# One stage in place of two at the head of a two-block transformer kernel: modulation product and first norm

## The reference, cut to what matters

```python
cond = jax.nn.silu(c)                      # c: 1 x 1024
mod = cond @ w_mod[l] + b_mod[l]           # w_mod: 1024 x 6144
shift_m, scale_m, gate_m, shift_f, scale_f, gate_f = [m[:, None, :] for m in jnp.split(mod, N_MOD, axis=-1)]
h = rms_norm(x, g_mix_norm[l]) * (1.0 + scale_m) + shift_m
x = x + gate_m * hybrid_mixer(h, positions, w_in[l], ...)
```

## Time and profile before

| | |
|---|---|
| median of 3 runs | 2143.41 us (2143.37 to 2143.73) |
| profiled execution | 2143.22 us, of which its span is 2141.5 us |
| `setup_stage`, from the span's start to the next stage's first instruction | 0 to 49.99 us |
| `norm_stage` mix1, in the same way | 49.99 to 72.01 us |
| `front1_stage`, in the same way | 72.01 to 213.06 us |

### The profile page before, as it was taken

The page is one execution under the profiler, slowest core; times in us unless marked ns, Lnnn a source line. Parts: engine busy times, 40 slices in busy tenths (PEclk is TensorE's granted clock), DMA queues, the critical chain, the costliest instruction groups (busy, mean ns, idle before and its releaser), DMA issues. The chain is left out here.

```text
span 2141.5 us, 28179 instructions
## 1 busy us (share of the span) xinstructions
PE 1873.8 (87%) x8588; PEld 1457.6 (68%) x8590; DVE 1321.0 (62%) x1543; ACT 1029.7 (48%) x1347; POOL 663.9 (31%) x510
## 2 busy tenths in 40 slices
PE   5778899997879999999999940789989878998999
PEld 2665676776758888888888830556666557887887
DVE  1692565454769999999999948364556654333332
ACT  0321344432248888888888831254555522222221
POOL 0498892000014666666666620011101100000000
PEclk9789899999689999999999975799999989999999
DMA  7644552211259999999999935432210003231222
GB/s 255 178 146 135 158 148 78 63 60 62 101 194 340 364 377 359 368 376 372 372 357 348 367 106 225 96 83 60 55 50 20 20 32 105 96 131 43 96 97 79
DMA packets 167507, 373.39 MB, mean 174 GB/s; under 512 B 39798, under 2 KB 77110, under 8 KB 158982
## 3 DMA queue, kind: packets, MB, share of 16 engines
q1 hardware_dynamic: 148614, 325.34, 44.2%
q0 software_dynamic: 18816, 47.04, 6.6%
HBM read 356.19 MB, written 29.23 MB: 180 GB/s over the span
## 5 line engine op out<-in xcount | busy, mean ns | idle before, releaser
L108 DVE TENSOR_TENSOR exp_parts<-exp_raw,exp_parts 128x2048 fp32r<-128x2048 f32 x194 | 439.3, 2291 | 57.6 <-ACT exp_parts L1872 57.2
L102 PE MATMUL ps<-exp_parts,xgT 128*128 128x512 f32 x1536 | 377.0, 401 | 7.6 <-DVE xgT L108 4.1
L1872 ACT CAST exp_parts<-exp_raw 128x2048 fp32r<-128x2048 f32 x194 | 369.0, 1918 | 14.9 <-PE ps L102 13.2
L102 PEld LDWEIGHTS ps<-exp_parts,xgT 128*128 128x128 f32 x1536 | 286.3, 190 | 77.3 <-issue 12.6
L102 PE MATMUL ps<-exp_parts,exp_hT 128*128 128x512 f32 x768 | 196.3, 405 | 2.7 <-DVE exp_hT L108 2.7
L102 PE MATMUL ps<-w_down_parts,hidden_parts 128*128 128x512 f32 x768 | 176.5, 392 | 7.1 <-DVE w_down_parts L108 7.1
L1767 POOL DMA_INDIRECT xg<-h_rows,row_index x63 | 147.4, 2340 | 108.9 <-issue 99.6
L102 PE MATMUL ps<-h4T,w_up_parts 128*128 128x512 f32 x768 | 175.8, 391 | 5.2 <-DVE w_up_parts L108 5.2
L102 PEld LDWEIGHTS ps<-w_down_parts,hidden_parts 128*128 128x128 f32 x768 | 145.7, 190 | 37.9 <-issue 7.5
L102 PEld LDWEIGHTS ps<-h4T,w_up_parts 128*128 128x128 f32 x768 | 145.2, 189 | 35.6 <-ACT w_up_parts L156 5.4
L102 PE MATMUL ps<-h3T,w_parts 128*128 128x512 f32 (+1 forms) x576 | 157.3, 427 | 11.7 <-DVE w_parts L108 11.7
(11 more groups left out here) (422 smaller groups left out, 3196.0 us busy)
## 6 DMA issues: line engine op xcount, KB each, us to landing
exp_raw<-in_w_exp_gate SPq DMA_DIRECT2D x130, 512.0 KB, 5.8
exp_raw<-in_w_exp_up SPq DMA_DIRECT2D x130, 512.0 KB, 7.5
exp_raw<-in_w_exp_down SPq DMA_DIRECT2D x64, 1024.0 KB, 7.6
w_up_raw<-in_w_up SPq DMA_DIRECT2D x15, 1024.0 KB, 5.2
w_down_raw<-in_w_down SPq DMA_DIRECT2D x15, 1024.0 KB, 5.0
yk<-y_rows SPq DMA_DIRECT2D x8, 1536.0 KB, 17.6
w_raw<-in_w_in SPq DMA_DIRECT2D x42, 256.0 KB, 3.4
modw<-in_w_mod SPq DMA_DIRECT2D x4, 2048.0 KB, 23.9
```

The lines of the kernel that those rows point to most:

```text
L102: mm = nc.tensor.matmul(out, left[a], right[b], start=start and i == 0, stop=stop and i == 2)
L108: return nc.vector.tensor_tensor(dst, x, high.bitcast(F32), ALU.subtract)
L1872: nc.scalar.copy(dst, src).then_inc(s_hi[kind], 1)
```

## The change

`setup_stage` is gone, and block 1's call of `norm_stage` is replaced by a new `setup_norm_stage`. What it does:

- The four `w_mod` slabs are loaded in the order scale, scale, shift, shift (`COLS`), each in four pieces of two row tiles (512 KB) with a semaphore of its own. TensorE waits for a piece, not for a slab. The masks (now waited for by ScalarE) and `fetch_front` stand behind the slabs on SyncE's queue.
- GpSimd's queue issues only the identity at once. It waits until the first slab has landed, then issues the bias and the gain, then (once the second slab's first piece is there) `x` and three small tables.
- ScalarE squares as soon as `x` is there; its scrap output goes to unused columns of `g.mod`. It converts the masks at the end of the stage.
- VectorE works by column halves of 512: bias add, gain fold and the four multiplications for each scale half, then for each shift half the bias add and four additions into `h`, which lies in the place of the first slab. After the first half's additions come the first half's four low parts.
- TensorE turns the first half's four blocks between the sixth and the seventh matmul of the last slab, into banks 4 to 7, and the second half's four behind the last slab, into banks 0 to 3.
- One barrier is left where there were two. Block 2's norms still use `norm_stage`.

```diff
-def setup_stage(g, io):
+def setup_norm_stage(g, io, hT, fetch):
     NS = 2 * D // 512
+    PIECE = 2
+    NPIECE = KD // PIECE
+    COLS = [D, D + 512, 0, 512]
...
+        h = w[:, 0].rearrange("p k n -> p (k n)").rearrange("p (t d) -> p t d", t=NT)
+        junk = g.mod[:, 2 * D:6 * D].rearrange("p (t d) -> p t d", t=NT)
...
+        def turned_bank(half, t):
+            return g.ps[:, (4, 0)[half] + t, :]
...
-            for i in range(NS):
-                sp.dma_start(w[:, i], wmod[:, :, i * 512:i * 512 + 512]).then_inc(s_w[i], 16)
+            for i, c in enumerate(COLS):
+                for j in range(NPIECE):
+                    k = PIECE * j
+                    sp.dma_start(w[:, i, k:k + PIECE], wmod[:, k:k + PIECE, c:c + 512]).then_inc(s_w[i][j], 16)
+            sp.dma_start(maskf[:], io["const_mask"]).then_inc(s_mask, 16)
+            fetch(sp)
 
         @block.gpsimd
         def _(pool):
...
+            pool.dma_start(g.ident[:], io["const_ident"]).then_inc(s_ident, 16)
+            pool.wait_ge(s_w[0][NPIECE - 1], 16)
+            pool.dma_start(g.mod[:, 0:2 * D], bcast_rows(io["b_mod"][:, 0:2 * D], 2 * D)).then_inc(s_bias, 16)
+            pool.dma_start(gain[:], bcast_rows(io["g_mix_norm"], D)).then_inc(s_gain, 16)
+            pool.wait_ge(s_w[1][0], 16)
+            pool.dma_start(g.x[:], io["x"][0].rearrange("(t p) d -> p t d", p=P)).then_inc(s_x, 16)
             pool.dma_start(g.tri[:], io["const_tri"]).then_inc(s_const, 16)
             pool.dma_start(g.iota[:], io["const_iota"]).then_inc(s_const, 16)
             pool.dma_start(g.ropec[:], io["const_rope"]).then_inc(s_const, 16)
+            pool.wait_ge(s_const, 48)
+
+        @block.tensor
+        def _(pe):
+            def turn(half, t):
+                pe.wait_ge(s_h, NT * half + t + 1)
+                for k in range(4):
+                    c = (4 * half + k) * P
+                    tr = nc.tensor.transpose(turned_bank(half, t)[:, k * P:k * P + P], h[:, t, c:c + P], g.ident[:])
+                tr.then_inc(s_turn, 1)
+
+            pe.wait_ge(s_cond, 1)
+            for i in range(NS):
+                for k in range(KD):
+                    if k % PIECE == 0:
+                        pe.wait_ge(s_w[i][k // PIECE], 16)
+                    mm = nc.tensor.matmul(g.ps[:, i, :], cond[:, k, :], w[:, i, k, :], start=k == 0, stop=k == KD - 1)
+                    if i == NS - 1 and k == KD - 3:
+                        pe.wait_ge(s_ident, 16)
+                        for t in range(NT):
+                            turn(0, t)
+                mm.then_inc(s_ps, 1)
+            for t in range(NT):
+                turn(1, t)
 
         @block.scalar
         def _(act):
...
+            act.wait_ge(s_x, 16)
+            for t in range(NT):
+                nc.scalar.activation(junk[:, t, :], g.x[:, t, :], ACT.Square, accum_out=stat[:, 0, t:t + 1]).then_inc(s_sq, 1)
+            act.wait_ge(s_ms, 1)
+            nc.scalar.activation(stat[:, 2, :], stat[:, 1, :], ACT.Sqrt).then_inc(s_sq, 1)
+            for half in range(2):
+                for t in range(NT):
+                    act.wait_ge(s_turn, NT * half + t + 1)
+                    nc.scalar.copy(hT[:, 0, 4 * half:4 * half + 4, t * P:t * P + P],
+                                   turned_bank(half, t).rearrange("p (k q) -> p k q", k=4)).then_inc(s_hi, 1)
+            act.wait_ge(s_mask, 16)
+            nc.scalar.copy(g.mask[:], maskf[:])
 
         @block.vector
         def _(dve):
...
+            dve.wait_ge(s_sq, NT)
+            v.tensor_scalar(stat[:, 1, :], stat[:, 0, :], 1.0 / D, EPS, ALU.mult, ALU.add).then_inc(s_ms, 1)
+            dve.wait_ge(s_sq, NT + 1)
+            link(v.reciprocal(stat[:, 1, :], stat[:, 2, :]))
+            dve.wait_ge(s_bias, 16)
+            dve.wait_ge(s_gain, 16)
+            for half in range(2):
+                scale, gains = g.mod[:, D + 512 * half:D + 512 * half + 512], gain[:, 512 * half:512 * half + 512]
+                dve.wait_ge(s_ps, half + 1)
+                link(v.tensor_tensor(scale, g.ps[:, half, :], scale, ALU.add))
+                link(v.scalar_tensor_tensor(gains, scale, 1.0, gains, ALU.add, ALU.mult))
+                for t in range(NT):
+                    ins = v.scalar_tensor_tensor(h[:, t, 512 * half:512 * half + 512], g.x[:, t, 512 * half:512 * half + 512],
+                                                 stat[:, 1, t:t + 1], gains, ALU.mult, ALU.mult)
+                link(ins)
+            for half in range(2):
+                shift = g.mod[:, 512 * half:512 * half + 512]
+                dve.wait_ge(s_ps, half + 3)
+                link(v.tensor_tensor(shift, g.ps[:, half + 2, :], shift, ALU.add))
+                for t in range(NT):
+                    rows = h[:, t, 512 * half:512 * half + 512]
+                    v.tensor_tensor(rows, rows, shift, ALU.add).then_inc(s_h, 1)
+                if half == 0:
+                    for t in range(NT):
+                        low(0, t)
+            for t in range(NT):
+                low(1, t)
...
-        norm_stage(g, "mix1", io["g_mix_norm"], hT, scale=g.mod[:, D:2 * D], shift=g.mod[:, 0:D], fetch=fetch_front)
+        setup_norm_stage(g, io, hT, fetch_front)
...
-            setup_stage(g, io)
```

More of the change, by code:

```diff
@@ L209, in setup_stage @@
         maskf = g.sb("maskf", [P, 5, 512], ctx=st)
+        gain = g.sb("mix1_gain", [P, D], ctx=st)
+        stat = g.sb("mix1_stat", [P, 3, NT], ctx=st)
+        h = w[:, 0].rearrange("p k n -> p (k n)").rearrange("p (t d) -> p t d", t=NT)
+        junk = g.mod[:, 2 * D:6 * D].rearrange("p (t d) -> p t d", t=NT)
         s_c = g.sem("c_loaded")
+        s_bias = g.sem("mod_bias_loaded")
+        s_ident = g.sem("ident_loaded")
         s_const = g.sem("const_loaded")
-        s_w = [g.sem(f"modw_loaded{i}") for i in range(NS)]
+        s_mask = g.sem("mask_loaded")
+        s_x = g.sem("x_loaded")
+        s_gain = g.sem("mix1_gain_loaded")
+        s_w = [[g.sem(f"modw_loaded{i}{j}") for j in range(NPIECE)] for i in range(NS)]
         s_sig = g.sem("cond_sigmoid")
@@ L215, in setup_stage @@
         s_ps = g.sem("mod_psum_ready")
+        s_sq = g.sem("mix1_squares_summed")
+        s_ms = g.sem("mix1_mean_square_ready")
+        s_h = g.sem("mix1_h_halves_ready")
+        s_turn = g.sem("mix1_turned")
+        s_hi = g.sem("mix1_high_ready")
         s_dve = g.sem("setup_dve_steps")
@@ L227, in _ @@
+            fetch(sp)
         @block.gpsimd
         def _(pool):
-            pool.dma_start(g.mod[:, 0:2 * D], bcast_rows(io["b_mod"][:, 0:2 * D], 2 * D)).then_inc(s_const, 16)
-            pool.dma_start(g.ident[:], io["const_ident"]).then_inc(s_const, 16)
+            pool.dma_start(g.ident[:], io["const_ident"]).then_inc(s_ident, 16)
+            pool.wait_ge(s_w[0][NPIECE - 1], 16)
+            pool.dma_start(g.mod[:, 0:2 * D], bcast_rows(io["b_mod"][:, 0:2 * D], 2 * D)).then_inc(s_bias, 16)
@@ L231, in _ @@
+            pool.dma_start(gain[:], bcast_rows(io["g_mix_norm"], D)).then_inc(s_gain, 16)
+            pool.wait_ge(s_w[1][0], 16)
+            pool.dma_start(g.x[:], io["x"][0].rearrange("(t p) d -> p t d", p=P)).then_inc(s_x, 16)
             pool.dma_start(g.tri[:], io["const_tri"]).then_inc(s_const, 16)
-            pool.dma_start(maskf[:], io["const_mask"]).then_inc(s_const, 16)
             pool.dma_start(g.iota[:], io["const_iota"]).then_inc(s_const, 16)
             pool.dma_start(g.ropec[:], io["const_rope"]).then_inc(s_const, 16)
-            pool.dma_start(g.x[:], io["x"][0].rearrange("(t p) d -> p t d", p=P)).then_inc(s_const, 16)
+            pool.wait_ge(s_const, 48)
@@ L242, in _, with low @@
+            act.wait_ge(s_mask, 16)
+            nc.scalar.copy(g.mask[:], maskf[:])
         @block.vector
         def _(dve):
+            v = nc.vector
             link = Chain(dve, s_dve)
+            def low(half, t):
+                dve.wait_ge(s_hi, NT * half + t + 1)
+                low_part(nc, hT[:, 1, 4 * half:4 * half + 4, t * P:t * P + P],
+                         turned_bank(half, t).rearrange("p (k q) -> p k q", k=4),
+                         hT[:, 0, 4 * half:4 * half + 4, t * P:t * P + P])
@@ L245, in _ @@
             dve.wait_ge(s_c, 16)
             dve.wait_ge(s_sig, 1)
[L247 to L265, removed]
+            link(v.tensor_tensor(g.cond[:], ccol[:, 0, :], ccol[:, 1, :], ALU.mult))
+            v.tensor_copy(cond[:], g.cond[:].unsqueeze(2).broadcast_to([P, KD, P])).then_inc(s_cond, 1)
@@ new lines, in _ @@
+            v.memset(g.ones[:], 1.0)
+            dve.wait_ge(s_ident, 16)
+            v.tensor_copy(g.identb[:], g.ident[:])
+            dve.wait_ge(s_sq, NT)
[13 more added lines that the diff above has]
+                link(ins)
```

## The result

The changed kernel takes 2125.9 us (median of 4 runs, 2118.56 to 2127.81), the kernel before 2143.57 us beside it (4 runs, 2143.37 to 2143.76): a ratio of 0.9918, 95% interval 0.99 to 0.9936. The forecast was 2127.8, range 2122.5 to 2133.5. The profiled execution of the changed kernel took 2127.81 us, with a span of 2126.1, so 15.4 us less than the 2141.5 of before. Its head ends 14.1 us earlier: `front1_stage` starts at 57.88 instead of 72.01.

What follows compares the result with a forecast made beforehand. The prediction took a serial head, with DMA at its limit, as the bound. Starting `front1_stage` at 56.4 instead of 72.0 saves 15.6 us: 2143.2 - 15.6 = 2127.6, adjusted by 0.2 to 2127.8 us; range 2122.5 to 2133.5.

Steps and rivals of the forecast that it cites:

- First slab seen: Loads at the head: first slab and identity, 2.17 MB, land at 8.9 us and are seen at 9.0.
- GpSimd's start-up of 4.0 us: GpSimd's load queue: data flow 4.0 us after issue, so the bias issued at 9.0 flows at 13.0.
- The 68% share: With both queues loading, GpSimd's gets 68% of the bandwidth, 0.272 MB/us, as queues take turns by packet.
- A: Rival, `x` starves: GpSimd's loads at an even share of bytes take 18.8 us instead of 13.5; 2133 us, chance 0.1.
- E: Rival, nothing gained: SyncE's queue is served to its end first, `x` lands at 41.7; 2142.7 us, chance 0.03.
- Scale halves: VectorE's bias add, fold, four multiplications and a link take 4.0 us a half; two halves end at 40.9.
- Turns and last products: TensorE at the head's end: four turns at half speed end at 46.2, two products then give `s_ps` at 48.7.
- B: Rival: GpSimd's start-up 2.0 instead of 4.0 us, and TensorE's clock stays up; together 2123.8 us, chance 0.2.
- C: Rival: TensorE's clock falls at the first trickling piece and stays at half, up to 3.5 us late; 2131.5 us, chance 0.05.
- Shift half 1 to the stage's end: Last head stretch: first block at 50.1, last 52.0, turn and copy 53.3, ScalarE's 2.4 us cast ends at 55.7.
- D: Rival, slower: VectorE's and TensorE's shifted work against GpSimd's lengthens `front1_stage` by over 15.6 us; chance 0.03.
- No later stage depends on the time of day: Stages behind the head: an earlier start ends them earlier by as much, so the head's saving arrives whole.

Runs made afterwards that it cites:

- e2_no_waits: Changed kernel with both of GpSimd's waits for slabs removed, so it issues all its loads at once: 2119.93 us, ratio 0.9921 to the kernel before.
- e5_x_first: Changed kernel with `x` issued right behind the identity, GpSimd's second wait gone, masks converted early: 2121.4 us, ratio 0.9896; `front1_stage` starts at 51.01.
- e10_wide_shift_rows: Changed kernel with both shift slabs loaded as one in 4 KB rows, the halves' products side by side: 2127.47 us, one execution; stage starts 3.1 us later.
- e8_filler: Changed kernel with five thrown-away products behind the last slab's sixth, against TensorE idling: 2128.87 us, one execution; `front1_stage` starts at 56.30.
- e3_masks_early: Changed kernel with ScalarE converting the masks between the root and its first copy: 2122.23 us, ratio 0.993; `front1_stage` starts at 55.61.
- e1_again: Changed kernel rerun without edit, 10 runs: 2127.68 us against 2137.03 for the kernel before (21 runs), ratio 0.9943; `front1_stage` starts at 57.53.
- e12_before_again: Kernel before, unchanged, profiled again beside the last experiments: 2129.9 us; `front1_stage` starts at 71.89.
- e6_x_by_halves: Changed kernel with `x` loaded as two column halves, meant to halve its packets: 2128.11 us, one execution; `front1_stage` starts at 57.82.

## Why the prediction was right

It forecast a head shorter by 15.6 us; it is shorter by 14.1. The profiled execution's span is shorter by 15.4, because the stages behind the head happened to be 1.3 us shorter in it. Point by point:

- **What sets the end.** The order forecast held at each link: `x`, squares, root, VectorE's halves, turns, the last two products, shift half 1, the cast, one barrier. `e2_no_waits` and `e5_x_first` show the links: move `x`, and the head moves until TensorE takes over.
- **First slab seen, 9.0 forecast, 10.32 measured.** The bytes came when they were forecast: the row below has 2.12 MB on SyncE's queue by 9.0, and the slab has 2.10. The sum took the time of that byte count for the one at which the waiting engine goes on, 1.3 us later. The profile has 7.1 us from the issue of the slab's last piece (2.92) to its landing, so to 10.02: 1.0 us lie between the count and the landing, 0.3 between the landing and GpSimd's next issue. The kernel before had the same gap (2.12 MB moved by 17.6, first product at 18.54), so it could have been read ahead. This is the largest error of the head, and it shifted all behind it. The queues of the changed kernel from 0 to 9 us:

```profile
q1 hardware_dynamic: 2132, 2.12, 75.9%
```

and its slab's last piece, L251 issued at 2.92:

```profile
DMA to landing us min/median/max: 7.1/7.1/7.1
```

- **GpSimd's start-up of 4.0 us.** Measured 4.0: issue at 10.32, no packet of its queue from 13 to 14.3, 7 packets from 14.3 to 14.4. The Trainium skill's 2.0 us for this path (page "DMA: Bandwidth & Descriptors", section "Anatomy of one DMA — SWDGE (gpsimd) path") falls short here as before.
- **`x` at 26.8, measured 28.53.** 1.3 us are the slab's, 0.4 the flow. The 68% share was right and is now shown, by `e10_wide_shift_rows`. A (even shares) and E are ruled out for this kernel: their marks, an `x` at 31 or later, weren't seen.
- **Root, 6.1 us,** measured 6.0 (28.53 to 34.53).
- **Scale halves, 8.0 us,** measured 8.5: the multiplications go at a pitch of 0.685 (2.74 / 4) instead of 0.61. That pitch came from L108, the low parts, which are another operation (TENSOR_TENSOR). The four additions of a shift half are of that kind and have a pitch of 0.62 (2.50 us for four); the four multiplications are SCALAR_TENSOR_TENSOR and do not. Shift half 0, 1.4 us to its first block, measured 1.56.
- **Turns and last products.** Half speed at the turns was a choice between two ends, and it was the right one, though not for the reason given. That reason was a TensorE half busy while pieces trickle in; the clock stayed at 1.00 through that stretch here. What came true is a wait of 6.58 us, longer than the 3.5 to 5.5 forecast because `x` was late, and the clock fell 3.8 us into it. With the forecast wait it could have gone either way. From the first turn to the sum of shift half 1 it gave 6.4 us, and it took 5.66 (44.57 to 50.23), since the transposes took 3.65 instead of 4.0 and the clock was up sooner. B's clock would have saved about 1.5 us (`e8_filler`), and wasn't seen. C has the clock fall at the trickling pieces. In the two profiles of the changed kernel it didn't. In `e3_masks_early` and `e8_filler`, whose loads are the same, it did (0.50 from 30 to 32 us in `e3_masks_early`), and it came up again by itself at about 33. The early products then ended at 40.0 (29.13 + 10.88) and 39.5 instead of 38.0, still 4 us ahead of VectorE's block. So the clock can fall where C has it fall, but in these two it didn't stay down, and it cost nothing because VectorE was the late one. (C's range, up to 46 against a first block at 42.3, makes 3.7 us and not the 3.5 written there; its time of 2131.5 has the 3.7.)
- **Shift half 1 to the stage's end, 7.0 us,** measured 6.8, with 2.33 for the cast (2.4).
- **Sum of the head.** +1.3 (first slab seen), +0.4 (flow), -0.1 (root), +0.5 and +0.2 (pitches), -0.7 (turns), -0.2 (shift half 1 and cast), +0.2 (0.87 from the cast's end to the next stage, instead of 0.7): 1.6, against the 1.5 us by which the stage starts later (57.88 against 56.4; the rest is rounding).
- **Behind the head.** D wasn't seen: `front1_stage` took 141.59 against 141.05. "The saving should arrive whole" holds for the head. "No later stage depends on the time of day" can't be upheld so simply: `front1_stage` has lengths of 138 and 141 us, the mixer behind it 318 and 321, the stage ahead of the experts 57 and 66, the MLP 381.5 and 384, in kernels where nothing there was edited. That the forecast total was met in the profiled execution is therefore luck; the median of the four runs lay 1.9 us under it.

Three things stay open. In `e1_again` the medians differ by 9.4 us where the head gives 14: ten of the 21 runs of the kernel before lay at 2130 to 2135.2 there, and none of the changed kernel's ten under 2124. If runs with the shorter stage ahead of the experts come less often once that stage starts earlier, the change loses part of its saving there; the changed kernel had one at 2118.56 in its first four, which may be such a run; it has no profile. Of the fourteen profiles, `e3_masks_early` and `e12_before_again` alone have the shorter stage. No experiment moved the head by waiting alone, so this isn't settled. Nor was it found what in a run decides how long TensorE's clock stays at 0.50 there, or whether it falls while the pieces trickle in.

## What to carry to other kernels

Merging two serial stages paid what the timeline said, and what is left to gain lies in the order of the loads: `x` issued ahead of the first wait, with the masks converted early, gave 6.9 us more at the head, although the cast then stood in the way of the first copies. The masks alone gave 1.1, while the pieces and the scale first gave nothing, and the pieces let TensorE finish early, idle, and turn at half clock. When a load is late, ask who issues it, behind what, and in what packets. Judge such edits by the start of the next stage in a trace, which repeated within 0.4 us in the two pairs of profiles of the same kernel (`x` landed up to 0.55 us apart between kernels with the same loads), and not by a total that varies by 10 us or more behind it.

## What the runs showed that I had not expected

- **Two lengths for the same stage.** The stage ahead of the experts ran 30 us with TensorE busy 28.4 of them at a clock of 0.50 in the changed kernel's window above (526 to 556), and at 0.96 in `e3_masks_early`. TensorE worked on with hardly a gap, and the clock came up only at about 560.6, more than 30 us into it. The Trainium skill, page "TensorE: Matmul & The Clock Gate", section "What's actually happening", says that activity releases the throttle; this stretch stands against it, or needs a condition more that no run here shows.
- **VectorE beside GpSimd.** 73 instructions of `front1_stage` cost 82.0 us in one run and 74.4 in another, and the stage was 3.8 us longer. Both engines had the same instructions to do. What differed is not shown; how the two engines' instructions lay against each other is a guess.
- **The queues shared by packets, and the two queues made packets of different size from the same runs.** GpSimd's queue made 3.9 KB packets even of 2 KB runs (`e6_x_by_halves`), SyncE's followed the run: 1.9 KB for 2 KB runs, 3.6 KB for 4 KB ones. So the length of the run set SyncE's share: 35% and 50% of the engines' time here.
- **The same trickle of work kept the clock in one execution and lost it in another.** In the changed kernel TensorE did two products from 23.9 to 29.15 us, with gaps of 1.56 and 1.68 us, and the clock stayed at 1.00. In `e3_masks_early` and `e8_filler` the gap ahead of the first of these products was 2.09 us, and the clock was at 0.50 a little after 26. Behind 38.0, with nothing to do, the changed kernel's clock fell after 3.8 us.
- **At the program's start the clock column doesn't tell TensorE's speed.** Two windows of the changed kernel are both at 1.00: from 6 to 9 us there are 4 matmul instructions in 3 us, from 30 to 38 us 19 in 8 us, of the same tiles. The weight loads between them start 0.86 us apart in the one (7.30, 8.16) and 0.43 in the other (30.11, 30.54).

```profile
6.00:9.00 3.00, 3.00 (x4) 1.01 (x3) 0.00 (x0) 0.00 (x0) 0.00 (x0) 1.00 1.04 384
```
